# Hybrid decoder block: the down projection by Strassen's seven products, with the sums of weight blocks made by GpSimd and kept in DRAM

## What is computed

```python
        h2 = rmsnorm(x, g_norm2[l]) * (1 + sc2) + sh2
        f_g, f_u = jnp.split(h2 @ w_gate_up[l], 2, axis=-1)
        x = x + gt2 * ((jax.nn.silu(f_g) * f_u) @ w_down[l])
    return rmsnorm(x, g_final)
```

## Time and profile before

| | |
|---|---|
| median of 3 runs | 987.19 us |
| the profiled execution | 986.81 us |
| its span in the trace | 985.0 us |
| end of gate and up on PE | 858.7 us |
| end of down on PE | 978.7 us |
| end of the span | 985.0 us |

### The profile page before, as it was taken

One profiled execution on the slowest core, in us unless ns is written; L12 is line 12 of the kernel. 1 busy time (PEld: TensorE's weight loads), 2 busy tenths in 40 slices (PEclk: granted clock), 3 DMA queues, 4 the chain that ended last, 5 costly groups with the idle time before them and its releaser, 6 DMA issues.

```text
span 985.0 us, 12729 instructions
## 1 busy us (share of the span) xinstructions
PE 969.2 (98%) x4913; PEld 802.9 (82%) x4913; DVE 494.0 (50%) x847; ACT 379.9 (39%) x685; POOL 117.4 (12%) x161
## 2 busy tenths in 40 slices
PE   7999999999999999999999999999999999999997
PEld 4778888878888977888788888988888888888886
DVE  4764778833457556465655555634334334321323
ACT  5355332255577766632222225432232222211322
POOL 1500000077023312100000011000000000000401
PEclk9999999999999999999999999999999999999999
DMA  8732845356335311264646651224443334232312
GB/s 329 241 123 86 275 131 167 111 169 221 97 89 170 114 33 44 74 226 139 214 138 214 246 171 43 78 73 124 146 148 114 106 106 149 86 110 83 129 43 86
DMA packets 91875, 134.13 MB, mean 136 GB/s; under 512 B 5464, under 2 KB 71605, under 8 KB 91698
## 3 DMA queue, kind: packets, MB, share of 16 engines
q1 hardware_dynamic: 89234, 120.18, 37.7%
q0 software_dynamic: 2448, 13.03, 4.1%
q10 hardware_dynamic: 144, 0.26, 0.1%
HBM read 125.01 MB, written 13.17 MB: 140 GB/s over the span
## 4 chain that ended last, share of the span: by engine, by line
PE 93%; issue 2%; POOL 2%; ACT 1%; DMA 1%; DVE 1%; SPq 0%; POOLq 0%; DVEq 0%
PE tile_ps L924 19%; PE tile_ps L925 18%; PE tile_ps L926 18%; PE t_ps L1194 2%; PE o_ps L1226 2%; PE tile_ps L1377 1%; PE s_ps L1377 1%; PE s_ps L1375 1%; PE t_ps L1377 1%; PE t_ps L1375 1%; PE tile_ps L1375 1%; PE tile_ps L1376 1%; PE s_ps L1376 1%; PE t_ps L1376 1%; PE s_ps L1179 1%
## 5 line engine op out<-in xcount | busy, mean ns | idle before, releaser
L924 PE MATMUL tile_ps<-h_hi,w_hi 128*128 128x512 f32 x736 | 291.1, 395 | 0.0
L925 PE MATMUL tile_ps<-h_lo,w_hi 128*128 128x512 f32 x736 | 286.9, 390 | 0.0
L926 PE MATMUL tile_ps<-h_hi,w_lo 128*128 128x512 f32 x736 | 286.7, 390 | 0.0
L1902 DVE TENSOR_TENSOR w_lo<-w_raw,w_hi 128x2048 fp32r<-128x2048 f32 (+3 forms) x60 | 130.7, 2179 | 155.2 <-ACT w_hi L1501 154.4
L924 PEld LDWEIGHTS tile_ps<-h_hi,w_hi 128*128 128x128 f32 x736 | 138.1, 188 | 36.1 <-issue 6.9
L926 PEld LDWEIGHTS tile_ps<-h_hi,w_lo 128*128 128x128 f32 x736 | 138.2, 188 | 29.4
L925 PEld LDWEIGHTS tile_ps<-h_lo,w_hi 128*128 128x128 f32 x736 | 138.3, 188 | 27.3 <-issue 0.2
L1501 ACT ACTIVATE w_hi<-w_raw 128x2048 fp32r<-128x2048 f32 (+3 forms) x60 | 107.3, 1788 | 40.8 <-DMA w_raw<-in_w_branch_c_dram 10.2
L1899 DVE TENSOR_TENSOR t_lo<-t_raw,t_hi 128x2048 fp32r<-128x2048 f32 (+1 forms) x15 | 32.7, 2183 | 85.6 <-ACT t_hi L1499 85.5
L1499 ACT ACTIVATE t_hi<-t_raw 128x2048 fp32r<-128x2048 f32 (+1 forms) x15 | 27.0, 1800 | 81.4 <-PE s_ps L1377 53.5
L1646 ACT ACTIVATE nl<-nl,cst 128x256 f32<-128x256 f32 (+3 forms) x81 | 42.6, 527 | 33.1 <-DVE cst L2106 33.0
(11 more groups left out here) (413 smaller groups left out, 1709.0 us busy)
## 6 DMA issues: line engine op xcount, KB each, us to landing
w_raw<-in_w_in_dram SPq DMA_DIRECT2D x31, 1024.0 KB, 6.0
w_raw<-in_w_gate_up_dram SPq DMA_DIRECT2D x22, 1024.0 KB, 7.3
ada<-in_w_ada_dram SPq DMA_DIRECT2D x12, 1024.0 KB, 5.3
t_raw<-in_w_down_dram SPq DMA_DIRECT2D x10, 1024.0 KB, 5.1
row_copies<-row_flat POOLq DMA_DIRECT2D x1, 5632.0 KB, 21.4
ada<-in_w_ada_dram SPq DMA_DIRECT2D x8, 640.0 KB, 11.5
tab<-masked_tables SPq DMA_DIRECT2D x8, 576.0 KB, 5.6
ada<-in_w_ada_dram SPq DMA_DIRECT2D x8, 512.0 KB, 4.7
```

What stands on the lines that cost most here:

```text
L924: pe.matmul(dst[0:mw, :], wh, x_hi[:, kx, :], start=start, stop=False)
L925: pe.matmul(dst[0:mw, :], wh, x_lo[:, kx, :], start=False, stop=False)
L926: mm = pe.matmul(dst[0:mw, :], wl, x_hi[:, kx, :], start=False, stop=stop)
L1902: dve.tensor_tensor(w_lo[s][:, 0:kt, 0:n_cols], w_raw[s][:, 0:kt, 0:n_cols], w_hi[s][:, 0:kt, 0:n_cols].bitcast(F32), ALU.subtract) \
```

## The change

Tokens are split in two halves of 256, the inner width in two halves of 11 row tiles, the columns in two halves of 512. With A the activation blocks and B the weight blocks, the kernel computes the seven products of Strassen's algorithm in Winograd's form in place of eight. Each product `p` has three chunks of 4, 4 and 3 row tiles, `n = 3p + c`, and two token blocks `t`: 24, 24 and 18 instructions.

- PE: 21 chunks. A product waits for its banks to be read. In the last two chunks the order is (19,t0), (20,t0), (19,t1), (20,t1). There are no quarters.
- POOL, new, beside gate and up (`load_down_rows`, `sum_down_rows`): for each of 11 pairs of row tiles a load of 1 MB, four sums of 128x512, a store of 1 MB to `wsum_dram`. ACT waits for the last store before it writes `a_hi`.
- SP: products 0, 3 and 6 load from `w_down`, the other four from `wsum_dram`.
- ACT and DVE: the activation is no longer split tile by tile in gate and up (`f_nat` stays whole). For each chunk ACT now makes `a_hi` (1024 or 768 columns) and `t_hi` (2048 or 1536), and DVE `a_lo` and `t_lo`. DVE also makes twelve block sums (`left_sum`) ahead of the low parts of chunks 2 to 10.
- Three products are copied out of PSUM by ACT (`copy_product`) and combined by DVE (`after_low`) and POOL. The right halves are squared by ACT inside the chunk loop, two before the high parts of chunk 20 and two after. POOL has 22 instructions of 128x512 after the products begin, where it had 8.

The sizes and the operands of a chunk:

```diff
+N_DN = 21
+DN_KTS = ((0, 4), (4, 8), (8, 11))
...
+        def left_of(n):
+
+            p, c, ks = dn_of(n)
+            return [f_part(c, 0, 0), a_sum[:, ks, :], a_dif[:, ks, :], a_all[:, ks, :], a_sum[:, ks, :],
+                    f_part(c, 1, 1), f_part(c, 1, 0)][p]
```

POOL, the sums of the weights and the combination of the products:

```diff
-            for b in range(NBLK):
-                pool.wait_ge(dn_read, b + 1)
-                pool.tensor_tensor(x1[:, b, 0:HW], gated2[b % 2][:], x1[:, b, 0:HW], ALU.add).then_inc(x2_half, 1)
...
+            def sum_down_rows(c):
+
+                w, t = wd_raw[c % 2], wd_sum[c % 2]
+                pool.wait_ge(wd_in, WD_IN + 16 * (c + 1))
+                if c + 1 < KH:
+                    load_down_rows(c + 1)
+                pool.tensor_tensor(t[:, 0, :], w[:, 0, HW:D], w[:, 0, 0:HW], ALU.subtract).then_inc(wd_summed, 1)
+                pool.tensor_tensor(t[:, 1, :], w[:, 1, HW:D], w[:, 0, HW:D], ALU.subtract)
...
+                pool.dma_start(wsum_dram[c], t[:]).then_inc(wd_stored, 16)
...
+            pool.wait_ge(p_copied, 6)
+            pool.wait_ge(dn_read, 4)
+            for t in range(2):
+                pool.tensor_tensor(p_seven[:, t, :], p_seven[:, t, :], p_one[:, t, :], ALU.add).then_inc(pool_seq, 1)
...
+            for t in range(2):
+                pool.tensor_tensor(x1[:, 2 + t, HW:D], x1[:, 2 + t, HW:D], p_five[:, t, :], ALU.add).then_inc(x2_half, 1)
+            for t in range(2):
+                pool.wait_ge(dn_read, 5 + t)
+                pool.tensor_tensor(x1[:, t, HW:D], x1[:, t, HW:D], gated2[t][:], ALU.add).then_inc(x2_half, 1)
```

PE, one chunk for one block of 128 tokens:

```diff
+            def down(n, t):
+
+                p, c, ks = dn_of(n)
+                bank = (t_ps, s_ps, tile_ps, s_ps, o_ps, tile_ps, t_ps)[p][t]
...
+                for k in range(kw):
+                    pe.matmul(bank[:], ah[:, k, tok], t_hi[s][:, k, :], start=first and k == 0, stop=False)
+                    pe.matmul(bank[:], ah[:, k, tok], t_lo[s][:, k, :], start=False, stop=False)
+                    mm = pe.matmul(bank[:], al[:, k, tok], t_hi[s][:, k, :], start=False, stop=last and k == kw - 1)
```

ACT, the high parts of a chunk and the order of the loop:

```diff
+            def dn_high(n):
+
+                p, c, ks = dn_of(n)
+                if n == 0:
+                    act.wait_ge(wd_stored, WD_STORED + 16 * KH)
+                if n >= 2:
+                    wait_dn_used(act, n - 2)
...
+                act.activation(a_hi[n % 2][:, 0:ks.stop - ks.start, :], left_of(n), ACT.Copy)
+                make_hi(CH_DN + n, (TL_GU + 41, TL_GU + 43)[n] if n < 2 else None, wide=ks.stop - ks.start)
...
+            for n in range(N_DN):
+                dn_high(n)
+                if n in (4, 7, 10):
+                    copy_product(n // 3 - 1)
+                if n >= N_DN - 2:
                     for q in range(2):
...
+                        m = 2 * (n - N_DN + 2) + q
+                        square_right(m, order[m])
```

DVE, the low parts, the combination after chunks 16 and 17, and the end:

```diff
+            def dn_low(n):
+
+                p, c, ks = dn_of(n)
+                kw, (b, u) = ks.stop - ks.start, use(CH_DN + n)
+                dve.wait_ge(w_hi_made[b], u + 1)
+                dve.tensor_tensor(a_lo[n % 2][:, 0:kw, :], left_of(n), a_hi[n % 2][:, 0:kw, :].bitcast(F32), ALU.subtract)
+                make_lo(CH_DN + n, wide=kw)
...
+                    if n == 16:
+                        dve.wait_ge(dn_made, 9 + t)
+                        dve.tensor_tensor(p_one[:, t, :], o_ps[t][:], p_one[:, t, :], ALU.add).then_inc(dn_read, 1)
+                    if n == 17:
+                        dve.wait_ge(dn_read, 3 + t)
+                        link(dve.tensor_tensor(gated2[t][:], gated2[t][:], p_one[:, t, :], ALU.add))
+                        dve.tensor_tensor(gated2[t][:], gated2[t][:], gate2_row[:, HW:D], ALU.mult).then_inc(dn_read, 1)
...
+            last_left(0)
+            finish(0, 2)
+            finish(1, 3)
+            last_left(1)
+            finish(2, 0)
+            finish(3, 1)
```

More of the change, by code:

```diff
@@ L882, in _ @@
+            pool.wait_ge(pool_seq, seq + 12)
+            for t in range(2):
+                pool.tensor_tensor(x1[:, 2 + t, 0:HW], x1[:, 2 + t, 0:HW], p_one[:, t, :], ALU.add).then_inc(x2_half, 1)
             pool.wait_ge(half2_sq, NBLK)
@@ new lines, in _ @@
+            for n in range(N_DN - 2):
+                p, c, ks = dn_of(n)
+                if c == 0 and p == 2:
+                    wait_tile_out(pe, TL_GU + 42)
+                    wait_tile_out(pe, TL_GU + 43)
+                if c == 0 and p == 4:
+                    pe.wait_ge(gate2_ready, 1)
+                if c == 0 and p in (3, 5, 6):
+                    pe.wait_ge(p_copied, {3: 4, 5: 6, 6: 2}[p])
+                chunk_ready(CH_DN + n)
+                for t in range(2):
+                    down(n, t)
@@ L1881, in _ @@
+            for n in range(2, NBLK):
+                square_left(n, order[n])
+                scale_right(n, order[n])
             act.wait_ge(o_done[0], NBLK)
-            act.dma_start(out[0, S - P:S, 0:HW], o_nat[:, NBLK - 1, 0:HW]).then_inc(stored, 16)
+            act.dma_start(out[0, P:2 * P, HW:D], o_nat[:, 1, HW:D]).then_inc(stored, 16)
         @block.vector
```

316 lines of the change are left out of this document (192 added, 124 removed).

## The result

The changed kernel takes **1012.06 us** (median of 4 runs, 1005.62 to 1014.67) against 986.91 us before on the same chip (4 runs, 986.48 to 987.54). The ratio is 1.0241, with a 95% interval of 1.0220 to 1.0262. So it is slower, by 25 us where I had forecast 16.5, and the median lies 2 us above the upper end of my range. The direction was right and the size was not.

A forecast was written before the change was run, and what follows sets the result against it. Down was taken as bound by the number of PE instructions. Last gain at 991.3 us, plus 7.3 for the end and 3.1 for the store, gave 1001.7; with 1.8 outside the span, 1003.4 us, range 992 to 1010.

The forecast's parts named there:

- port term: End of down: POOL and DVE hold each other up, 37.4 us from POOL's start on the combining to the last gain.
- Part 1: PE in down: 462 instructions of 0.2267 us take 104.7 us in place of 120.0, a gain of 15.3 us.
- Part 2: Down: PE waits for ACT and DVE to split, 2.7 us at the start of products 1 to 6; sum 19.4 us.
- Part 3: End of down: POOL and DVE exclude each other, DVE first back to back; 37.4 us, PE waiting some 8 before chunk 20.
- Part 4: The end behind the last gain: 7.3 us for root, finish and last block, then 3.1 us for the store.
- What is hidden, gate and up: POOL's 44 additions there can delay a low part by 1.3 us at a time, with 5.3 us spare: no cost.
- Rival 4: The clock falls behind the 8 us wait before chunk 20: 1003.4 to 1005.4 us, inside the forecast's range; no separate chance.
- rival 2: End of down: POOL is served first, low parts of chunk 17 wait up to 7 us: 1010 us; 10%.

The follow-up runs named there:

- e_dma_last_fill: The changed kernel with POOL's load of the next weight row issued behind the additions, and dummy matmuls in PE's waits before products 1 to 6: 1005.97 us.
- e_narrow_fill: The changed kernel with POOL's 18 operations on the products cut to 1 column (output wrong) and five dummy matmuls before each of products 1 to 6: 995.99 us.
- e_a3: The changed kernel with a third buffer for the activation blocks, so ACT and DVE split the next chunk's block earlier: 996.09 us.
- e_dma_last: The changed kernel with POOL's load of the next weight row issued behind a row's additions and store, not in front: 1008.96 us.

## Why the prediction was wrong in size

The forecast's sum had two costs at nothing that the runs show. POOL's additions in gate and up can hold up a low part where PE has no time to spare, and the clock falls behind short waits of PE. Here is the sum, step by step, against e_dma_last_fill, which has neither stall nor fallen clock in its waits, and its profiled run (1005.72 us):

| step | forecast | measured | difference |
|---|---|---|---|
| start of down | 858.7 | 859.5 | +0.8 |
| to POOL's start on the combining | 95.2 | 95.8 | +0.6 |
| port term, to the last gain | 37.4 | 36.3 | -1.1 |
| last gain to the last store | 7.3 | 7.9 | +0.6 |
| store to the end of the span | 3.1 | 4.3 | +1.2 |
| outside the span | 1.8 | 1.9 | +0.1 |

Together +2.2. On top of that come 3.0 us for the clock, and 6 to 7 us for the stall in some runs. 1006.0 + 3.0 = 1009.0 without the stall, and 6.5 more is 1015.5 with it. The four runs of the changed kernel lie at 1005.6 and 1009.7, and at 1014.4 and 1014.7. The sum meets three of them within 1.1 us; the run at 1005.6 has no profile and shows no price of the clock, and why is open. The median of 1012.06 is the middle of the two inner runs, so it was partly chance that it lay outside my range: with one upper run fewer it would have been near 1010.

- **Part 1**, 15.3 us saved on PE: held. Parts 1 and 2 together gave PE's end within 1.4 us in e_narrow_fill.
- **Part 2**, the splitting chain: held, waits of 2.4 us for 2.5 (2.7 with the 0.2 for a weight load, which the waits do not show), 1.5 for product 2, and the cause is shown by e_a3. That a wait of this size costs only itself was the silent assumption in it.
- **Part 3**, the port term: the size held (37.4 forecast, 38.3 measured in the changed kernel, 11.2 against 10.0 us by taking it away), and partly by luck. The rule "back to back DVE is served first" failed. They take turns. The row that I built it on fits turns better: POOL's 2.77 us are 1.43 over the group's median of 1.34, which is one DVE subtraction (1.47) and not the two. With turns the long wait came two chunks earlier, behind DVE's four short additions. ACT's two squares in front of chunk 20, which I had made its cause, started at 971.9 right behind the high parts of chunk 19 and cost nothing. And of the 38.3 us POOL worked or stood for DVE 29.4, where I had 37.4; the rest were the waits for DVE's sum and for ACT's last squares, the second of them behind PE (in e_dma_last_fill, with the clock full, POOL waited 0.2 us for the squares and not 2.3).
- **Part 4**: the end was 0.6 us longer, and the store 4.2 to 4.3 us in the changed kernel and all ten experiments where the earlier trace rows had 3.1. Why is open.
- **What is hidden, gate and up**: this step failed. I wrote that POOL's additions can delay a low part by 1.3 us at a time, against 5.3 us to spare. Three additions and the remainder of a DMA issue held one up by 4.2 us, in the first round of gate and up where less than 1 us was to spare (PE waited 3.4 of the 4.2), and the fallen clock cost about as much again. It makes the upper group. I had read the slack in one round and POOL's series (one DMA issue and three additions without a pause between them) not at all.
- **Rival 4**, the clock: this failed too. I priced it for one wait of 8 us in front of chunk 20 and let it lie inside the range. It fell behind two waits of 2.3 and 2.4 us as well as behind the long one, and cost 3.0 us. The row that I had the earlier trace rows showed it falling within 4 us of a stop; six waits of 2.7 us beside that row should have carried a price of their own.
- **The range** ended at 1010, rival 2's time. It had no case in which two things outside my sum came together, and two did.

The late start of down is not of the change: in e_narrow_fill PE began it at 858.6, in the changed kernel at 859.9. The difference is there before POOL's first new instruction (631.0 us): the low part that DVE starts at 619.4 us in the kernel before starts at 619.2 in e_narrow_fill's profile and at 620.5 in the changed kernel's.
